# Feed-forward of a two-block model: up projection in seven block products a pair, gated activations through memory, down projection in one pass

## The reference

```
h2 = rmsnorm(x, norm2_g) * (1 + scale2) + shift2
u  = h2 @ w_up                      # 1024 x 1024 by 1024 x 5632
a, g = split(u, 2)                  # 2816 columns each
a  = conv_w[0] * a[t-2] + conv_w[1] * a[t-1] + conv_w[2] * a[t] + conv_b
x  = x + gate2 * ((gelu(a) * g) @ w_down)     # 1024 x 2816 by 2816 x 1024
out = rmsnorm(x, final_g)
```

## Time and profile before

| | |
|---|---|
| median of 3 timed runs | 2838.17 us (2837.12 to 2841.01) |
| the profiled execution | 2832.38 us, of it 2830.6 us from first to last instruction (the span) |
| TensorE busy / mean granted clock | 2677.3 us, 95% / 0.978 |
| DVE, ACT, POOL busy | 1310.7, 860.8, 844.2 us |
| feed-forward, from its four first units to the end | about 2091 to 2830.6 us of the span |

### The profile page before, as it was taken

The page is one execution under the profiler, slowest core; times in us unless marked ns, Lnnn a source line. Parts: engine busy times, 40 slices in busy tenths (PEclk is TensorE's granted clock), DMA queues, the critical chain, the costliest instruction groups (busy, mean ns, idle before and its releaser), DMA issues.

```text
span 2830.6 us, 33366 instructions
## 1 busy us (share of the span) xinstructions
PE 2677.3 (95%) x12783; PEld 2235.0 (79%) x12783; DVE 1310.7 (46%) x1726; ACT 860.8 (30%) x1481; POOL 844.2 (30%) x594
## 2 busy tenths in 40 slices
PE   3899999999899999999999988869999999999998
PEld 2688888788778899977888878658778888888877
DVE  5666665630433566647300007844466413541444
ACT  3300012511410788846111017751252101110111
POOL 1133331022232666600233230232002333333335
PEclk7899999999999999999999999989999999999999
DMA  5245443353355644432433136212221111111113
GB/s 212 89 135 152 134 141 109 90 193 105 141 199 158 134 105 105 98 127 77 162 134 128 51 86 153 75 55 95 82 68 52 45 53 45 53 45 53 45 51 121
DMA packets 318268, 293.98 MB, mean 104 GB/s; under 512 B 32756, under 2 KB 264605, under 8 KB 317853
## 3 DMA queue, kind: packets, MB, share of 16 engines
q1 hardware_dynamic: 308348, 254.61, 31.2%
q10 hardware_dynamic: 9760, 37.23, 3.4%
HBM read 241.98 MB, written 49.81 MB: 103 GB/s over the span
## 4 chain that ended last, share of the span: by engine, by line
PE 84%; DVE 8%; ACT 3%; DMA 3%; issue 1%; POOL 1%; SPq 0%; DVEq 0%; ACTq 0%; POOLq 0%
PE PS L1393 63%; PE PS L623 5%; PE PS L1437 4%; PE PS L601 2%; PE PS L1460 2%; DMA mod_raw<-in_w_ada 1%; PE PS L587 1%; PE PS L586 1%; PE PS L1508 1%; DVE M L1923 1%; PE PS L746 1%; PE PS L706 1%; DVE w_lo L2021 1%; DVE prob L977 1%; PE PS L686 1%
## 5 line engine op out<-in xcount | busy, mean ns | idle before, releaser
L1393 PE MATMUL PS<-opA,w_hi 128*128 128x512 f32 x4544 | 1417.9, 392 | 19.1 <-POOL w_lo L1234 13.7
L1393 PEld LDWEIGHTS PS<-opA,w_hi 128*128 128x128 f32 x4544 | 859.5, 189 | 201.3 <-POOL w_lo L1234 16.1
L1393 PE MATMUL PS<-opA,w_lo 128*128 128x512 f32 x2272 | 889.0, 391 | 0.0
L1229 POOL CAST w_hi<-w_raw 128x1024 fp32r<-128x1024 f32 (+1 forms) x174 | 180.6, 1038 | 1583.5 <-PE PS L1393 1145.0
L1393 PEld LDWEIGHTS PS<-opA,w_lo 128*128 128x128 f32 x2272 | 430.0, 189 | 89.2 <-issue 0.2
L1234 POOL TENSOR_TENSOR w_lo<-w_raw,w_hi 128x1024 fp32r<-128x1024 f32 (+1 forms) x176 | 425.8, 2419 | 86.6 <-ACT w_hi L1711 72.6
L1393 PE MATMUL PS<-opB,w_hi 128*128 128x512 f32 x1216 | 381.1, 392 | 7.2 <-POOL w_lo L1234 4.4
L1393 PEld LDWEIGHTS PS<-opB,w_hi 128*128 128x128 f32 x1216 | 229.6, 189 | 56.8 <-POOL w_lo L1234 4.8
L1923 DVE SCALAR_TENSOR_TENSOR M<-mod_raw,small,M 128x512 f32<-128x512 f32 x168 | 169.8, 1011 | 172.7 <-DMA mod_raw<-in_w_ada 90.1
L1393 PE MATMUL PS<-opB,w_lo 128*128 128x512 f32 x608 | 237.7, 391 | 0.0
L2204 DVE SCALAR_TENSOR_TENSOR X<-PS,mod,X 128x512 f32<-128x512 f32 x96 | 72.1, 751 | 278.0 <-PE PS L1393 276.9
(11 more groups left out here) (193 smaller groups left out, 3077.9 us busy)
## 6 DMA issues: line engine op xcount, KB each, us to landing
mod_raw<-in_w_ada SPq DMA_DIRECT2D x96, 256.0 KB, 3.0
w_raw<-in_w_up SPq DMA_DIRECT2D x44, 512.0 KB, 3.8
w_raw<-in_w_in SPq DMA_DIRECT2D x34, 512.0 KB, 3.9
w_raw<-in_a_w_in SPq DMA_DIRECT2D x32, 512.0 KB, 4.9
q_dram<-stage ACTq DMA_DIRECT2D x16, 1024.0 KB, 4.0
hin<-q_dram SPq DMA_DIRECT2D x64, 256.0 KB, 6.0
k_dram<-stage ACTq DMA_DIRECT2D x13, 1024.0 KB, 4.2
mod_raw<-in_b_mod_w SPq DMA_DIRECT2D x48, 256.0 KB, 2.8
```

Source lines behind the costliest of these rows:

```text
L1229: pool.tensor_copy(hi, raw).then_inc(pool_done, 1)
L1393: ins = pe.matmul(ps, w[:, k0 + k, :], rhs(part, k0 + k), start=(k == 0 and n == 0), stop=(k == chunks - 1 and n == 2))
```

## The change

Two of the 22 tiles (0 and 1, the four quad units) are worked as before. The other 20 (`SEVENS`) are worked as pairs: the a row of weights and the g row, each in two halves of the 1024 input features (A11, A12 for a, A21, A22 for g), against the tokens in two halves and the same two feature halves (B11, B12 in the first feature half for tokens 0 to 511 and 512 to 1023, B21, B22 in the second). In place of the 8 block products of 12 matmuls there are 7 (Winograd's form of Strassen's rule), in the order P1 = A11 B11, P2 = A12 B21, P6 = (A21 + A22 - A11)(B22 - B12 + B11), P5 = (A21 + A22)(B12 - B11), P7 = (A11 - A21)(B22 - B12), P4 = A22 times a sum of all four B, P3 = (A12 minus P6's weights) B22. Products are added in PSUM where they can be; P1, P1 + P6 and P1 + P6 + P7 are needed more than once, so ACT copies them out (`snap`), and DVE adds four block sums.

The sums of weights are made by POOL for each pair (`weight_sums`, 4 of 128x512), the sums of tokens by POOL once (`token_sums`, 16 of 128x512, from h2 that is now kept in `opB`). High parts of all are made by ACT (`weight_high`, `token_high`), low parts by DVE (`weight_low`, `token_low`). Sums of weights and the parts of five of the seven lie in `X`; so x goes to memory first (`spill_half`) and comes back during the down projection (`reload_last`). The last convolution tap that ACT can make (the tap without shift, with the bias) moves from DVE to ACT (`first_tap`, Identity with scale and bias), the multiplication by g reads SBUF (`gated`). z goes to memory, high and low part (`z_store`, two DMAs of 512 KB a tile, issued by ACT).

The down projection follows in one pass: all of the first half's 24 units (3 groups by 8 output blocks, all 8 PSUM banks accumulating over the groups), then the second half, block by block. Each of the 48 units has one half. z comes back by `z_load`, in the places that earlier groups have left, issued by SP between the weight loads. `X` gets one update per half. The gains are loaded at unit U_DOWN + 24.

```diff
-    for first, many in FGROUPS:
-        for f in ffn_order(first, many):
-            units += both("w_up_2", [f * P, D_FF + f * P])
...
+    units += both("w_up_2", [P, D_FF + P, 0, D_FF])
+    units += [("w_down_2", n * P, first * P, many, (0,)) for first, many in FGROUPS for n in range(KC)]
+    units += [("w_down_2", n * P, first * P, many, (1,)) for n in range(KC) for first, many in FGROUPS]
...
+            def weight_sums(i):
+                a11, a12, a21, a22 = (seven_raw(i, r, k) for r in range(2) for k in range(2))
+                for which, in0, in1, op in ((P5, a21, a22, ALU.add), (P6, seven_sum(P5), a11, ALU.subtract),
+                                            (P7, a11, a21, ALU.subtract), (P3, a12, seven_sum(P6), ALU.subtract)):
+                    pool.wait_ge(seven_in[i % 2], at("seven_in", i))
+                    if i:
+                        pool.wait_ge(dve_done, at("seven_w", i - 1, which))
+                    else:
+                        pool.wait_ge(x_half[1], at("x_half", 1))
+                        pool.wait_ge(dve_done, at("xn", "n2", 2 * KC - 1))
+                    pool.wait_ge(pool_done, now(pool_done))
+                    pool.tensor_tensor(seven_sum(which), in0, in1, op).then_inc(pool_done, 1)
...
+            def token_sums():
+                for c in range(QK):
+                    pool.wait_ge(dve_done, at("lo", "n2", KC + QK + c))
+                    for which, out_of, in0, in1 in ((P5, b11, b12, b11), (P7, b12, b22, b12), (P6, b22, b22, b11),
+                                                    (P4, b21, b21, b22)):
+                        pool.tensor_tensor(out_of, in0, in1, ALU.subtract).then_inc(pool_done, 1)
...
+            def sevens(i):                                   # TensorE
+                f = i + 2
+                pe.wait_ge(act_done, at("snap", f - 2, 2) if i >= 2 else at("fa", i, 0))
+                products(P1, True, False)
+                products(P2, True, True)
+                pe.wait_ge(act_done, at("snap", f, 0))
+                products(P6, False, False)
+                pe.wait_ge(dve_done, at("fu", f - 2, 0, 1) if i >= 2 else at("fz", i, 0))
+                products(P5, True, False)
+                pe.wait_ge(act_done, at("snap", f, 1))
+                products(P7, False, True)
+                products(P4, True, True)
+                pe.wait_ge(dve_done, at("fu", f, 1, 1))
+                products(P3, False, True)
...
+            def token_low(which, c):                         # DVE
+                dve.wait_ge(act_done, at("token_hi", which, c))
+                if which in (P5, P6):
+                    dve.wait_ge(pool_done, at("token_sum", P6 if which == P5 else P4, c))
...
+            for c in range(QK):                              # ACT, first pair
+                token_high(P5, c)
+                token_high(P6, c)
+            weight_high(0, P1)
+            weight_high(0, P2)
+            first_copies(*CLASSIC[0])
+            for hf in range(2):
+                gelu(0, hf)
+            for hf in range(2):
+                z_high(0, hf)
+            for c in range(QK):
+                token_high(P7, c)
+            snap(0, 0)
...
+            for i in range(1, SEVENS):                       # ACT, later pairs
+                f = i + 2
+                snap(i, 0)
+                weight_high(i + 1, P1)
+                weight_high(i, P3)
+                gelu(f - 1, 1)
+                z_high(f - 1, 1)
+                weight_high(i + 1, P2)
+                first_tap(f, 0)
+                z_store(f - 1)
+                snap(i, 1)
+                weight_high(i + 1, P6)
+                gelu(f, 0)
+                weight_high(i + 1, P5)
+                snap(i, 2)
+                weight_high(i + 1, P7)
+                weight_high(i + 1, P4)
+                z_high(f, 0)
+                first_tap(f, 1)
...
+            for c in range(QK):                              # DVE, first pair
+                token_low(P5, c)
+                token_low(P6, c)
+            weight_low(0, P1)
+            weight_low(0, P2)
+            first_conv(*CLASSIC[0])
+            first_product(*CLASSIC[0])
+            for hf in range(2):
+                z_low(0, hf)
+            for c in range(QK):
+                token_low(P7, c)
+            first_conv(*CLASSIC[1])
+            for c in range(QK):
+                token_low(P4, c)
+            weight_low(1, P1)
+            weight_low(1, P2)
+            block_sum(2, 0, 0)
+            weight_low(1, P6)
+            first_product(*CLASSIC[1])
+            for hf in range(2):
+                z_low(1, hf)
+            other_taps(2, 0)
+            for i in range(SEVENS):                          # DVE, all pairs
+                f = i + 2
+                if i:
+                    other_taps(f - 1, 1)
+                    weight_low(i + 1, P1)
+                    weight_low(i, P3)
+                    gated(f - 1, 1)
+                    block_sum(f, 0, 0)
+                    z_low(f - 1, 1)
+                    weight_low(i + 1, P2)
+                    other_taps(f, 0)
+                    weight_low(i + 1, P6)
+                weight_low(i + 1, P5)
+                block_sum(f, 1, 1)
+                weight_low(i + 1, P7)
+                block_sum(f, 1, 0)
+                gated(f, 0)
+                weight_low(i + 1, P4)
+                z_low(f, 0)
+                block_sum(f, 0, 1)
...
+                if U_DOWN + 2 <= u < U_DOWN + 6:             # SP, behind weights(u)
+                    for k in range(2 * (u - U_DOWN - 2), 2 * (u - U_DOWN - 1)):
+                        z_load(0, 1, k)
...
+                if u == U_DOWN + 24:
+                    row_gains()
-                if u == U_LAST:
-                    sp.wait_ge(pe_done, at("unit", U_LAST - 1, 1))
-                    sp.dma_start(g_row[:], a["final_g_2"].rearrange("(o d) -> o d", o=1).to_broadcast([P, D])).then_inc(g_in, 16)
...
+            for g in range(3):                               # TensorE
+                for n in range(KC):
+                    down(0, g, n)
+            for n in range(KC):
+                for g in range(3):
+                    down(1, g, n)
```

More of the change, by code:

```diff
@@ new lines, in down @@
+            def down(hf, g, n):
+                u = down_unit(hf, g, n)
+                s, chunks = u % 2, FGROUPS[g][1]
+                pe.wait_ge(pool_done, at("split", u))
+                if hf == 0 and g == 0:
+                    pe.wait_ge(dve_done, at("fz", FC - 2, 1) if n < 4 else at("fu", FC - 1, 0, 1))
+                if hf == 1 and g == 0:
+                    pe.wait_ge(dve_done, at("x_new", "fin2", n - 2, 1) if n >= 2 else at("x_new", "fin2", n * 2 + 5, 0))
+                for k in range(chunks):
+                    if n == 0:
+                        if (hf, g) in ((0, 0), (1, 1)):
+                            pe.wait_ge(z_chunk[k], at("z_in", hf, g, k))
+                        else:
+                            pe.wait_ge(z_group[hf, g], at("z_in", hf, g, chunks - 1))
+                    for m, (w, part) in enumerate(((w_hi, 0), (w_lo, 0), (w_hi, 1))):
+                        ins = pe.matmul(PS[:, down_bank(hf, n), :], w[:, s, k, :], z_operand(hf, g, part, k),
+                                        start=(g == 0 and k == 0 and m == 0), stop=(g == 2 and k == chunks - 1 and m == 2))
+                ins.then_inc(pe_done, 1)
+                step(pe_done, "unit", u, hf)
+                names[("unit", u, 1 - hf)] = names[("unit", u, hf)]
@@ new lines, in gelu, with z_high @@
+            def gelu(f, hf):
+                act.wait_ge(dve_done, at("fconv", f, hf))
+                act.wait_ge(act_done, now(act_done))
+                act.activation(yt[:, hf, :], yt[:, hf, :], ACT.Gelu).then_inc(act_done, 1)
+                step(act_done, "fg", f, hf)
+            def z_high(f, hf):
+                act.wait_ge(dve_done, at("fz", f, hf))
+                if f >= 2:
+                    act.wait_ge(z_stored[f % 2], at("z_stored", f - 2))
+                else:
+                    act.wait_ge(pe_done, at("unit", U_FFN + 1, 1))
+                act.wait_ge(act_done, now(act_done))
+                act.activation(z_part(f, 0, hf), yt[:, hf, :], ACT.Copy).then_inc(act_done, 1)
+                step(act_done, "fh", f, hf)
@@ new lines, in first_tap @@
+            def first_tap(f, hf):
+                act.wait_ge(dve_done, at("fu", f, 0, hf))
+                act.wait_ge(dve_done, at("fl", f - 1, hf))
+                act.wait_ge(act_done, now(act_done))
+                w, b = C["conv_w_2"] + 2 * FC + f, C["conv_b_2"] + f
+                act.activation(yt[:, hf, :], M[0][:, hf * HALF:(hf + 1) * HALF], ACT.Identity, bias=cols[:, b:b + 1],
+                               scale=cols[:, w:w + 1]).then_inc(act_done, 1)
+                step(act_done, "ft", f, hf)
@@ new lines, in _ @@
+            first_copies(*CLASSIC[1])
+            for c in range(QK):
+                token_high(P4, c)
```

(38 more changed lines are left out.)

375 lines of the change are left out of this document (279 added, 96 removed).

## The result

The changed kernel takes 2811.43 us (median of 4 runs, 2809.30 to 2812.67); the kernel before took 2837.64 beside it (4 runs, 2831.68 to 2841.01). The ratio is 0.9909, with a 95% interval of 0.9891 to 0.9927. The forecast was 2811.7.

What follows compares the result with a forecast made beforehand. TensorE alone was taken to bound the stage: 62.1 us taken out, less 30.2 (start), 3.4 (steady pairs) and 2.0 (down projection), gives 26.5 less, 2811.7 us from a median of 2838.17. Own range 2800 to 2824; with rivals 2797 to 2843.

Steps and rivals of the forecast that it cites:

- The gains' wait: Last down-projection group: TensorE's wait behind the output gains' load (4.6 us) and its slow clock (3.1) go, 7.7 us saved.
- The start: First pair: TensorE waits for POOL's sums and the DVE and ACT queues behind them; 30.2 us lost, range 20 to 38.
- The walk: Operation-by-operation count of engine queues: first-pair waits 29.2 us with the second pair's 1.3; steady pair 0.2 us late at P7.
- The slow clock: First pair: clock losses behind waits fall mostly into time waited for anyway; 1.0 us added.
- The steady pair: Later pairs: P7 waits for ACT's second copy, 0.2 us a pair, 17 times, 3.4 us lost; the least sure term.
- the other outcome: Rival in each pair: POOL's fourth sum goes before DVE's gating, 21.6 us more, 2833 us; chance 0.18.
- The spill: X's move to memory ahead of the pairs: said to lie beside matmuls, no cost counted.
- The down projection: First half: added z and X traffic brings some units' weights late; 2.0 us lost, from 0 to 31.
- No exclusion: Rival in the pairs: POOL and DVE do not hold each other up; start 20, steady 0, 2798 us; chance 0.12.
- Table loads: Rival on ACT: Identity taps between Gelus force table loads, 4.05 us a pair, 73 us, 2881 us; chance 0.04.
- POOL twice a pair: Rival: POOL delays DVE at gating and P4's weight low part, 2.6 us a pair, 47 us, 2855 us; chance 0.08.
- DMA at 230 GB/s: Rival: the down projection becomes bound by DMA, 29 us more, 2841 us; chance 0.08.

Runs made afterwards that it cites:

- tokens_dve: Changed kernel with the first pair's 16 token sums computed by DVE in place of POOL; median 2802.41 us.
- fewer_lows: Changed kernel with spill later, token sums on DVE, second copy before z stores, and without DVE's eight token low parts for P7 and P4; 2791.04 us, output wrong.
- snap_first: Changed kernel with ACT's second copy of a pair ahead of the two DMA issues of z; median 2809.38 us.
- pool_first: Changed kernel with DVE's gating made to wait for POOL's fourth weight sum in each pair; median 2835.25 us.
- splits_later: Changed kernel with POOL's first two down-projection weight splits held back to the end of the last pair's P7; median 2808.57 us.
- spill_later: Changed kernel with the spill of X's first half moved beside the second half's, behind the quad units' weight loads; median 2814.91 us.
- z_copied: Changed kernel with 7 MB of extra z copies by DMA in the down projection's first half; median 2828.54 us.

## Why the prediction was right, and where it was not

**Taken out.** 240 matmuls: right. The profile has 640 + 560 + 480 = 1680 of the seven products, at the old pitch: 54.4. The gains' wait: 7.7 forecast (0.17 of it counted twice), 7.1 when it alone was moved, and the changed kernel shows no trace of it.

**The start: 30.2 forecast, 28.2 measured**, from the end of the quad units (2136.02) to the start of the second pair (2183.24), less 19.04. Its mechanism held: the same waits in the same order, with the releasers named, and the token sums on POOL ahead of DVE's queue as a part of the cause: moving them to DVE takes 6.5 of 21.9 us out of the waits (tokens_dve). Two terms in it were mis-sized, and that they nearly cancel is luck. The waits were put at 29.2; they are 10.4, 5.7 and 5.8, with 0.17 more each by the length of a record 22.5. P1's was 11.7 and is 10.4 because the quad units end later; without the spill it is 12.0. P6 and P7 were forecast 2.6 and 1.1 too late and the second pair 1.3. The walk let matmuls run at full rate, and slower products leave less to wait for: that is 1.4 of the 2.6 at P6 (the rest is not accounted for), and the slow P6 (1.8) and P3 (2.6) are longer than what was to be waited for behind them. The slow clock was put at 1.0 and is 28.2 - 22.5 = 5.7: P1 and P2 took 7.04 us for 24 matmuls that need 5.6, and the 12 of P3 took 5.3 in place of 2.7, at a granted clock of 0.50. That such losses "fall mostly into time that is waited for anyway" was right for the products ahead of a wait and wrong for P3, behind which nothing waits: fewer_lows shows that P3 runs at 1.00 when its wait is 2.8 and not 6.0.

**The steady pair: 0.2 a pair forecast, 0.20 measured**, and at the wait that was named (snap_first). But the match in size is luck. The walk had the copy 0.2 late; it is 0.06 late in the mean. The other 0.15 is what P7's first matmuls lose behind any wait, which the prediction didn't have; and it is 15 pairs, 3.2 us, not 17. Among the walk's terms the two DMA issues last 1.19, not 0.85, and start while the first tap still runs, so that both take 1.53 in place of 1.78. That DVE would start its gating ahead of POOL was a choice between rows 0.1 us apart; it came true by 0.03, in every pair, and pool_first shows that the other outcome was priced rightly (21.6 forecast, 23.2 measured, and some slow clock at the end).

**The last pair: nothing forecast, 2.9 measured.** The step that failed is the sentence on the down projection that POOL's first two splits "wait for P1 and P2 of the last pair and end long before its P3". They do; but the exclusion of POOL and DVE, which the prediction applied to the weight sums, applies to these splits as well, and there it was not counted (splits_later).

**The spill: nothing forecast, 2.8 measured** at the quad units, 1.5 of it a later start and 1.3 the lower clock behind it. That "the spill of X lie beside matmuls" looked at TensorE and not at the DMA engines: 2 MB issued 5 us ahead of the weights that the quad units start on. By spill_later it costs the end 0.2 to 1.8, the rest being taken out of the wait at P1.

**The down projection: 2.0 forecast, 1.1 measured**: 244.8 us from the sevens to the last down unit, against 1056 x 0.2267 and 4.3 for the small matmuls between. 0.7 of it are the one wait at 2671, for weights: a sign that the prediction had named for being wrong here, and it came, at a size below the term. The bound is near, as 0.89 of busy time says and z_copied shows.

**The sum.** 54.4 + 7.7 - 28.2 - 3.2 - 2.9 - 2.8 - 1.1 = 23.9, against 23.5 measured in the stage. The forecast's 26.5 is 3 too much: 5.7 for the two terms it didn't have, less 2.0, 0.2 and 0.9 for those that it had too large; 0.4 stay open. That the medians differ by 26.2 and not by 23.5 lies within the scatter: the four runs of the kernel before beside this one span 9.3 us.

**The rivals.** No exclusion: ruled out by the rows of 1.80 and 1.82. Table loads: 40 Identity taps of 0.817 us and one table load among them and the Gelus, so the rule of the Trainium skill (ScalarE: Activation LUTs, Table sets: the hidden batching unit) that the prediction cited holds for Identity too. POOL twice a pair: pairs last 19.24 and not 21.6; POOL's second sum does hold the low part of P7's weights (the 1.80), but off the path that ends last. DMA at 230 GB/s: the first half moved 296. (That rival's 31 us count a MB as 10^6 bytes; in units of 2^20, as in the 5.1 us a unit, they would be 38.)

## What to carry to other kernels

A change that takes 240 of 3168 matmuls out of a stage gave back more than half of what that saves in places where the engines around TensorE start up, hand over or end: price the first and the last round of a new loop by themselves, with every operation that another stage has queued beside them. Where two engines exclude each other, apply that to each pair of operations that can meet, those of the next stage too. A loss ahead of a wait is free until the wait goes: fix the wait first, then measure the loss again. And where a sum comes out right, check its terms: the start and the steady pair were right here in the sum only.

## What the runs showed of the hardware

- The same wait doesn't always cost the same clock. Behind the wait in the last pair the next 36 matmuls took 8.46 us in the changed kernel (2.9 us idle, granted clock 1.00), and 10.06 and 10.10 in spill_later and tokens_dve (2.8 each, mean granted clock 0.83).
- A wait costs more than its idle time at full clock, too: the first matmuls behind it lose 0.13 to 0.18 us at a granted clock of 1.00, whether TensorE stood for 0.02 us (the changed kernel's P7) or for 1.4 (pool_first, where 24 matmuls take 5.75 us in place of 5.60).
- POOL and DVE stretch each other both ways: POOL's token sums took 1.26 to 1.62 us beside DVE's low parts, its casts 1.29 in place of 1.04, DVE's subtracts up to 2.71.
- DMA moved 336 GB/s at a share of 1.00 with weights, rows of 2 KB and copies within memory mixed, more than the 313 of the mix in the earlier trace rows.
